# The memory of both layers projected in the expert groups, and the first block's start reordered

## What is computed

```python
def reference(x, meta_tokens, ...):
    x = first_block(x, meta_tokens, ...)     # 1 layer
    return second_block(x, mem_2, ...)       # 2 layers, LAYERS in the kernel

def first_block(...):
    h = concatenate([meta, x])               # 16 + 256 tokens of width 1024
    a = rms_norm(h, norm_mix)
    p = a @ w_in                             # 1024 x 4096
    y_hy = hyena_mixer(p[..., :1536], ...)   # short conv, filters from a small sine network, FFT conv
    y_hg = hgrn2_mixer(p[..., 1536:], ...)
    h = h + concatenate([rms_norm(y_hy, ...), y_hg]) @ w_out
    h = h + hier_moe(rms_norm(h, norm_ffn), ...)   # 64 experts, each token uses 2
    return rms_norm(h, norm_final)[:, 16:]

def hyena_filter_spectra(L, w1, b1, w2, b2, w3, freq):
    hid = sin(freq * (z @ w1 + b1))
    hid = sin(freq * (hid @ w2 + b2))
    filt = (hid @ w3).reshape(L, 2, 2, 512) * window
    ...                                      # forward and backward parts joined, then rfft

def hybrid_layer(x, mem, ...):               # second_block runs it for l = 0 and l = 1
    proj = rms_norm_2(x, norm_pre) @ w_in    # five branches and their gates
    ...
    mkv = rms_norm_2(mem, mem_norm) @ w_mem_kv     # 256 memory tokens, 1024 x 1024
    mem_k, mem_v = split(mkv, 2)
    y_xa = memory_attention(xa_q, mem_k, mem_v)
    ...
```

## Time and profile before

| | us |
|---|---|
| median of 3 runs (lowest to highest) | 2370.54 (2368.7 to 2375.32) |
| the profiled execution | 2367.8 |
| its span | 2366.0 |
| TensorE busy in the span | 2004.5 (85%) |
| TensorE loading weights | 1359.0 (57%) |
| VectorE busy | 891.0 (38%) |
| ScalarE busy | 279.7 (12%) |
| first block up to the first expert group's products | 0 to 327.8 |
| experts | to 1258 |
| layers 0 and 1 | to the end |

### The profile page before, as it was taken

The page is one execution under the profiler, slowest core; times in us unless marked ns, Lnnn a source line. Parts: engine busy times, 40 slices in busy tenths (PEclk is TensorE's granted clock), DMA queues, the critical chain, the costliest instruction groups (busy, mean ns, idle before and its releaser), DMA issues. The chain is left out here.

```text
span 2366.0 us, 24364 instructions
## 1 busy us (share of the span) xinstructions
PE 2004.5 (85%) x10176; PEld 1359.0 (57%) x10176; DVE 891.0 (38%) x1479; ACT 279.7 (12%) x624; POOL 0.2 (0%) x4
## 2 busy tenths in 40 slices
PE   7999976667676666666668999999999999999998
PEld 5576843223232222222224888788885877788887
DVE  5446521111111111111113455465543244466553
ACT  1102210000000000000002221210002222110001
POOL 0000000000000000000000000000000000000000
PEclk9999988988978888888889999999999999999999
DMA  6121289999999999999996233434444234434442
GB/s 229 71 97 70 93 362 426 428 428 427 427 419 428 429 429 428 429 429 429 428 429 247 99 151 125 151 134 160 142 178 162 107 143 160 129 111 161 149 145 89
DMA packets 45819, 596.12 MB, mean 252 GB/s; under 512 B 5568, under 2 KB 7009, under 8 KB 8041
## 3 DMA queue, kind: packets, MB, share of 16 engines
q1 hardware_dynamic: 43672, 585.01, 61.6%
q10 hardware_dynamic: 2064, 9.91, 1.3%
HBM read 591.75 MB, written 1.06 MB: 251 GB/s over the span
## 5 line engine op out<-in xcount | busy, mean ns | idle before, releaser
L514 PE MATMUL ps<-arena,ring 128*128 128x256 f32 x1856 | 413.4, 378 | 0.2
L514 PEld LDWEIGHTS ps<-arena,ring 128*128 128x128 f32 x1856 | 345.8, 189 | 50.3 <-issue 3.4
L1585 PE MATMUL ps<-ring,arena 128*32 128x512 f32 x2048 | 251.0, 636 | 95.0 <-DMA ring<-in_w_experts 75.6
L717 PE MATMUL ps<-arena,ring 128*128 128x256 f32 x1280 | 289.2, 378 | 0.0
L1612 PE MATMUL ps<-ring,arena 128*32 128x512 f32 x1024 | 173.0, 809 | 113.3 <-DMA ring<-in_w_experts 105.8
L717 PEld LDWEIGHTS ps<-arena,ring 128*128 128x128 f32 x1280 | 241.5, 189 | 35.6 <-issue 1.0
L1585 PEld LDWEIGHTS ps<-ring,arena 128*32 128x32 f32 x2048 | 63.4, 114 | 262.6 <-issue 141.5
L1612 PEld LDWEIGHTS ps<-ring,arena 128*32 128x32 f32 x1024 | 32.6, 130 | 237.0 <-DMA ring<-in_w_experts 160.6
L723 PE MATMUL ps<-arena,ring 128*128 128x256 f32 x640 | 151.8, 379 | 0.3 <-DVE arena L956 0.2
L1572 PE MATMUL ps<-arena 128*128 128x128 f32 x512 | 91.2, 361 | 67.2 <-DVE arena L2118 67.2
L1170 DVE RECIPROCAL arena<-arena 128x256 f32<-128x256 f32 x80 | 140.3, 1754 | 2.8
(11 more groups left out here) (380 smaller groups left out, 1772.1 us busy)
## 6 DMA issues: line engine op xcount, KB each, us to landing
ring<-in_w_experts SPq DMA_DIRECT2D x192, 2048.0 KB, 25.5
ring<-in_w_layers SPq DMA_DIRECT2D x42, 2048.0 KB, 7.8
ring<-in_w_layers SPq DMA_DIRECT2D x40, 1536.0 KB, 6.6
ring<-in_w_first SPq DMA_DIRECT2D x10, 2048.0 KB, 8.0
arena<-in_w_mem SPq DMA_DIRECT2D x2, 2048.0 KB, 11.2
arena<-in_mem ACTq DMA_DIRECT2D x2, 1024.0 KB, 7.1
ring<-ml_rows_out ACTq DMA_DIRECT2D x2, 1024.0 KB, 4.8
ring<-arena ACTq DMA_DIRECT2D x4, 512.0 KB, 14.2
```

The costliest lines, as they stand in the source:

```text
L514: last = pe.matmul(ps[:, j % 2, 0:SEQ], t[:, s, k, :], lhs[:, k, :], start=(k == 0), stop=(k == KD - 1))
L717: last = pe.matmul(ps[:, j % 2, 0:SEQ], t[:, k, :], an[:, k, :], start=(k == 0), stop=(k == KD - 1))
L1585: last = pe.matmul(ps[CAP * e:CAP * (e + 1), v // 4, :], xg[:, (v % 4) * 2 + k, CAP * e:CAP * (e + 1)], w[:, k, e, :], start=(v % 4 == 0 a ...
```

## The change

1. Layer 1's memory weights (two units of 2 MB) leave the layers' stream and are loaded to `mem_w` behind the units of expert groups 3 and 5. PEELED goes from 6 to 12; groups 6 to 11 each do one of layer 1's memory jobs. SyncE's first six groups are written out too. Layer 1 has no `mem_k` and `mem_v` of its own any more, and no `mem_t`; the second load of the memory goes.
2. VectorE multiplies the memory by 1/rms in four steps of two tiles, in place; ScalarE applies the gains: `mem_t0` beside the output projection, layer 1's `mem_t1` (to the place of `an`) behind the four pieces of `xn` and ahead of the routing's exponentials. SyncE loads units 4 and 5 first and then waits for both before the memory weights.
3. At the start the constants are loaded later, the first weights in four quarters. Strips 0 to 3 take tokens multiplied by the gain alone (`gained`), and VectorE multiplies their results by 1/rms (`take_raw`). VectorE adds the eight squares, so that TensorE sums them in one product, with ones made on the chip.
4. The filter products run in three lots of four, with strips 4, 5 and 6 behind them. The short convolutions of strips 0 and 1 lie between VectorE's lots, those of strips 2 and 3 behind L1846's work.

```diff
-PEELED = NH + 2
+PEELED = LAYERS * (NH + 2)
...
-                if l:
-                    pe.wait_ge(sem("mem_n"), KD)
-                    project("mem_k", mem_t)
...
-                if l:
-                    project("mem_v", mem_t)
...
-            for v in range(4):
+            for v in range(RING):
                 expert_unit(v, 0, 0)
             sp.wait_ge(sem("mem_t0"), KD)
+            sp.wait_ge(sem("mem_t1"), KD)
             for i in range(2):
                 sp.dma_start(mem_w[i], d["w_mem"][i]).then_inc(sem("in_mem_w"), 16)
...
+            for g in range(1, NH + 2):
+                for v in range(12):
+                    expert_unit(v, g, g * 12)
+                if g == NH - 1:
+                    sp.wait_ge(sem("mem_ps"), NH)
+                    sp.dma_start(mem_w[0], d["w_mem"][2]).then_inc(sem("in_mem_w"), 16)
+                if g == NH + 1:
+                    sp.wait_ge(sem("mem_ps"), NH + 2)
+                    sp.dma_start(mem_w[1], d["w_mem"][3]).then_inc(sem("in_mem_w"), 16)
...
-            pe.wait_ge(sem("sq_mix"), 1)
-            pe.wait_ge(sem("in_const"), 16)
-            norm_sum(pe, ones, a, KD, ps[:, 3, 0:T], sem("ss_mix"))
+            strip(0)
             pe.wait_ge(sem("in_feat"), 48)
             pe.matmul(ps[0:64, 2, 0:T], fw1[0:33, :], zT[0:33, :], start=True, stop=True).then_inc(sem("hid"), 1)
-            pe.wait_ge(sem("normed_mix"), KD)
-            strip(0)
+            pe.wait_ge(sem("sq_mix"), 1)
+            pe.matmul(ps[:, 3, 0:T], ones_early, sum_sq, start=True, stop=True).then_inc(sem("ss_mix"), 1)
+            strip(1)
+            strip(2)
             pe.wait_ge(sem("hid_act"), 1)
             pe.matmul(ps[0:64, 2, 0:T], fw2[0:64, :], hid[0:64, :], start=True, stop=True).then_inc(sem("hid"), 1)
-            for n in range(1, 4):
-                strip(n)
+            strip(3)
...
+                if tt == 0:
+                    pe.wait_ge(sem("normed_mix"), KD)
+                strip(RAW + tt)
+            strip(LEAD - 1)
...
+            for k in range(KD):
+                act.activation(an[:, k, :], mem_first[:, k, :], ACT.Copy, scale=P2(1, "mem_norm", k)).then_inc(sem("mem_t1"), 1)
             act.wait_ge(sem("route_arg"), 1)
...
+            def take_raw(j):
+                dve.wait_ge(sem("strip"), j + 1)
+                dve.tensor_tensor(padded[:, j, 1:T + 1], strip_at(j), rstd, ALU.mult).then_inc(sem(f"strip_out{j % 2}"), 1)
...
+            for k in range(KD):
+                dve.tensor_scalar(gained[:, k, :], h[:, k, :], P1("norm_mix", k), None, ALU.mult).then_inc(sem("gained_mix"), 1)
+            for k in range(1, KD):
+                dve.wait_ge(sem("squares"), k + 1)
+                ins = dve.tensor_tensor(sum_sq, a[:, 0, :] if k == 1 else sum_sq, a[:, k, :], ALU.add)
...
+            filter_angle(0)
+            dve.wait_ge(sem("rstd_mix"), 1)
+            take_raw(0)
+            take_raw(1)
...
+            for k in range(KD):
+                dve.tensor_tensor(a[:, k, :], gained[:, k, :], rstd, ALU.mult).then_inc(sem("normed_mix"), 1)
+            take_raw(2)
+            filter_angle(1)
+            take_raw(3)
...
+                if tt < 2:
+                    short_conv(tt)
```

More of the change, by code:

```diff
@@ L340, in __init__ @@
             def __init__(self, l, unit_base, job_base):
-                groups = [g for g in UNIT_GROUPS if l or g not in MEM_GROUPS]
+                groups = [g for g in UNIT_GROUPS if g not in MEM_GROUPS]
                 self.l, self.unit_base, self.job_base = l, unit_base, job_base
@@ L389, in build_program @@
         mem_k0, mem_v0 = kept.take(4, SEQ), kept.take(2, HALF)
+        kv_at = kept.at
         mem_t0 = kept.take(KD, SEQ)
+        kept.at = kv_at
+        mem_k1, mem_v1 = kept.take(4, SEQ), kept.take(2, HALF)
         r_mem = ly.at
-        mem_t = ly.take(KD, SEQ)
+        ly.take(KD, SEQ)
         ml_qk = arena[:, r_mem:r_mem + 8 * SEQ]
@@ L399, in build_program @@
         ly.take(KD, SEQ)
-        mem_raw = ly.take(KD, SEQ)
+        rt_v = ly.take(2, HALF)
         la = Layout(arena, r_two)
@@ L979, in layers_dve @@
                 link(dve.tensor_scalar(keyneg, C("keymask"), BIG, -BIG, ALU.mult, ALU.add))
[L980 to L984, removed]
+                if l == 0:
                     dve.wait_ge(sem("final_r"), 1)
@@ L1257, in build_program @@
         block = block_one.enter_context(nc.Block())
+        m6 = Layout(ring[:, RING - 3, :])
+        gained = m6.take(KD, T)
+        ones_early = m6.take(P)
+        eps_early = m6.take(1)
+        sum_sq = m6.take(T)
         def job_evacuated(eng, j):
@@ L1759, in _ @@
             for c in range(KD):
+                for k in range(2 * c - 8, 2 * c - 6) if c >= 4 else ():
+                    act.wait_ge(sem("mem_hat"), c - 3)
+                    act.activation(mem_t0[:, k, :], mem_first[:, k, :], ACT.Copy, scale=P2(0, "mem_norm", k)).then_inc(sem("mem_t0"), 1)
                 job_evacuated(act, WOVEN + c)
@@ L1846, in _ @@
                 dve.scalar_tensor_tensor(fwd, fwd, 2.0, bwd, ALU.mult, ALU.subtract).then_inc(sem("filt_sd"), 1)
-            for j in range(4, LEAD):
+            for j in range(2, LEAD):
                 short_conv(j)
@@ L2037, in _ @@
                 if 3 <= c < 7:
-                    for k in (2 * c - 6, 2 * c - 5):
-                        dve.scalar_tensor_tensor(mem_t0[:, k, :], mem_first[:, k, :], P2(0, "mem_norm", k), hn_mem, ALU.mult, ALU.mult).then_inc(sem("mem_t0"), 1)
+                    m = mem_first[:, 2 * c - 6:2 * c - 4, :]
+                    dve.tensor_tensor(m, m, hn_mem.unsqueeze(1).to_broadcast([P, 2, SEQ]), ALU.mult).then_inc(sem("mem_hat"), 1)
             def sm(i, n=8):
@@ L2226, in layout @@
                 at = 0 if n == "mem_k" else w
-                (parts if l else memory).append(units(strips(kv[:, at:at + w])))
+                memory.append(units(strips(kv[:, at:at + w])))
             else:
```

123 lines of the change are left out of this document (61 added, 62 removed).

## The result

| | before | after |
|---|---|---|
| median, us (runs) | 2370.25 (2368.70 to 2375.32, 4) | 2351.70 (2346.97 to 2353.50, 4) |
| the profiled execution | 2367.8 | 2350.42 |
| its span | 2366.0 | 2348.3 |
| spectra start (L1373, now L1381) | 60.82 | 55.96 |
| last product of the router's scores | 307.78 | 303.07 |

The ratio is 0.992, with a 95% interval of 0.9907 to 0.9933: 18.6 us faster, where 22.7 were forecast. The stretches not listed (layer 0 behind its logits, the turn to layer 1, the tail) agree within 0.1 us. The differences of the table from the first group on add up to -3.36 + 10.23 + 0.08 (last down projection to layer 0's `gm_v`) + 1.55 + 0.76 - 25.00 - 1.99 = -17.7 us, which is the difference of the spans.

A forecast was written before the change was run, and what follows sets the result against it. Transfers were taken to bound the experts, TensorE the layers. Terms -26.0 + 9.8 + 0.3 + 1.3 - 8.1 = -22.7 us gave 2345.1 for the profiled execution, 2347.5 as median; range 2340 to 2355.

The forecast's parts named there:

- Rival A: Start: filter products or `take_raw` wait on VectorE's strict order, spectra near 57, start only -4, total 2351.6; chance 0.12.
- Layer 1, -25.0 for the stretch: Layer 1, first logits to attention on the memory: falls from 65.80 to layer 0's 40.81 us without the six jobs.
- Rival B: Layer 1: without the six jobs another chain stands bare, so only about -21 is kept, total 2352.5; chance 0.05.
- Layer 1, -1.0 for the rotation's wait: Layer 1's retention: a 1.81 us wait for the rotation may go or stay; 1.0 us taken off.
- The experts, +9.8 + 0.3: Expert groups: two more units at 4.90 us in a gapless stream, +9.8; loading written-out code, +0.3.
- Rivals D and E: D: groups 6 to 11 wait for new code, 2399, chance 0.02; E: TensorE 1.4 us late each, 2356, chance 0.05.
- The router, +1.3: Router: eight more ScalarE products ahead of the routing's exponentials start group 0 1.3 us later, counted in full.
- The start, -8.1 up to the spectra: Start: the reordered strips and filter lots let the spectra begin at 52.7 us and not 60.8.
- VectorE's chain of 8.2: Start: VectorE's work from the end of L1837 to the end of L1846, 8.2 us, which the spectra wait for.
- The 5.5: Start: strip 0, as the first work, takes 5.5 us and not 3.7, ending at 13.0.

The follow-up runs named there:

- peel_only: Kernel before with twelve expert groups written out on TensorE and ScalarE and six on SyncE, memory jobs left where they were; one execution, 2371.32 us.
- front_only: Kernel before with only its start changed (parts 3 and 4); median 2360.88 us over 10 runs, ratio 0.9968.
- peel_loads: Kernel before with the same groups written out, plus layer 0's two memory units loaded again, unused, behind groups 3 and 5; one execution, 2383.26 us.
- warm_start: Changed kernel with 22 unused products of 128x128 on TensorE ahead of strip 0; median 2349.96 us over 4 runs, ratio 0.9908.

## Why the forecast came out as it did

The forecast of 2347.5 was 4.2 us low. The measured 2351.70 lies in the range of 2340 to 2355, but 0.7 outside the 2343.5 to 2351 that got the chance of 0.66. Rival A's total, 2351.6 from -18.6, is the measured one almost to the digit; that is luck, as the steps show:

- **Layer 1, -25.0 for the stretch: right** to 0.01 us, and so was reading it from layer 0. Rival B falls: no further chain stands bare.
- **Layer 1, -1.0 for the rotation's wait: wrong in its cause.** In this execution 1.99 went; but kernels that leave layer 1 alone lose it too (`peel_only`, `front_only`, `peel_loads`), and it is back in two profiles with the change. One row of one execution had been taken for a property of the kernel. No run shows that the change gains anything here.
- **The experts, +9.8 + 0.3: right, a little low.** 10.2 in the profile, 10.4 for the loads alone between `peel_loads` and `peel_only`. The mean over eleven profiles with the loads is 933.2, over three without 921.8: 11.4. Rivals D and E fall: groups with new code and jobs move 427 to 428 GB/s. The 358 GB/s that the Trainium skill (DMA: Bandwidth & Descriptors, Specifications) gives as one core's share did not fit the trace, and the measurement decided; another page of the Trainium skill (HBM Reference, Specifications (TRN2)) says that a core streaming alone measures about 425 GB/s, and the 428 here agree with that.
- **The router, +1.3: right in this pair** (1.35 from the last scores to group 0). Over all profiles it looks smaller: 20.02 to 20.52 in the four without the change's order, 20.80 to 21.62 in the eight with it, 20.17 and 20.56 in the two with the exponentials first. The means of the first two groups differ by 0.9, and the order accounts for nearly all of it.
- **The start, -8.1 up to the spectra: the step that failed, -4.86.** Strip 0 began at 8.25 (7.5 in the forecast) and took 6.92 (5.5), so that the hidden layer behind it began at 15.10 and not 13.0: 2.1 of the 3.3 us. The `gained` tokens did not hold it up (VectorE had them all at 8.41). The strips up to the first lot and the hidden layer came within 0.3 of what was built. The lots and strips took 3.64 and 3.88 in place of 3.5 and 3.7, since I had rounded down: 0.6 by the last lot. VectorE's chain of 8.2 was exact (47.50 to 55.70), and so was its being what the spectra wait for. Rival A gave nearly the size of the loss, spectra near 57, but not its cause: VectorE's order held, TensorE stood for it nowhere ahead of the spectra, and what was late was TensorE's first strip. The 5.5 had been copied from a strip that came behind other products, where the granted clock was 0.67 on average (18 to 23 us); here nothing stood before it. In `front_only` it took 5.50, in the five profiles of the changed start with the memory part and without early products 6.28 to 6.97, with `warm_start` 3.93.
- **What no step had: the clock behind pauses.** In the profile after, the scan near 200 us lost 1.66 (the row at 200.11 took 6.87, 5.90 before), the output projection won 1.61 and the two `gm_v` lost 1.55 and 0.76: +2.4. So -22.7 + 3.2 (start) + 2.4 (clock) + 0.2 (experts, router) - 1.0 (rotation) = -17.9, and the spans differ by -17.7.

That the start, taken alone, gave 8.5 and not 4.9 is no proof of the forecast's build-up. The profiled `front_only` (span 10.0 under the kernel before; it ran 3.0 under its own median) reached its spectra at 53.97, 6.85 earlier, because its strip 0 began 0.6 sooner than in the kernel after and took 1.4 less. The rest is mainly the output projection at 3.26 instead of 4.87, a short expert stretch (920.0) and the rotation's wait that was not there; layer 0's `gm_v` took 1.5 back. The right total came partly from terms that were not in the sum.

## What to carry to other kernels

Read a stretch that will remain from its twin without the work that goes (layer 0 for layer 1) instead of adding up rows of the work. That was exact, where a sum of rounded rows missed 0.6 us over six of them, and a wait read from one execution turned out to be chance. Before a sum of parts is trusted to better than 5 us, list the places where TensorE starts again behind a pause of 1 us and more, with the time of their first products at both clock levels: each is a term that can come or go with any edit, and products that nothing uses, put into the pause, take it out of the sum and can save time. They have to end before the awaited data come (the five ahead of layer 0's `gm_v` made it start 1.07 us late here), and a gain in one place is no proof of a shorter kernel: `warm_start` won 3.5 us up to group 0 and its profile ended where the changed kernel's did.

## What the runs showed of the hardware

- Pauses of 1.5 and 2.6 us were enough for 1.2 GHz behind them in some executions (4.95 and 5.63 us for the first products) and not in another of the same kernel (3.26 and 3.95). Behind the 3.0 and 5.5 us ahead of the two `gm_v` the first products lost time in every profile, 15.4 to 17.0 us, against 13.97 to 14.00 with products in the pause (15.67 once).
- At the very start the recorded granted clock is no guide. The row of 8 to 12 us of the kernel after, columns as in the earlier trace rows, says 1.00, while strip 0's products came at half their later pace:

```profile
8.00:12.00 4.00, 3.75 (x8) 2.86 (x9) 3.42 (x9) 0.50 (x2) 0.00 (x0) 1.00 1.09 372
```

  Eight entries in 3.75 us are 0.47 each; a later strip has 3.93 / 16 = 0.25. In `warm_start` the same stretch, also with 1.00 on record, holds 18 entries. That the slow pace is the clock's is therefore concluded from the products put ahead, not read from the record.
- Six more groups of code written out in place of a loop, 0.18 MB, behind a queue that is never empty, made the expert stretch 0.85 us longer in the one pair of profiles that differs in it alone.
